# Stick-breaking attention: the order of two steps on ScalarE and of two on TensorE

## The chip, the cores and the metric

The kernel runs on one core of a Trainium2 chip. The time is the device time of one launch in microseconds, as the median of several runs. A core has five engines that run side by side, each through its own list of instructions in order: TensorE (matrix products; PE in the profile, PEld for its weight loads), VectorE (DVE), ScalarE (ACT), GpSimd (POOL) and SyncE (SP, which starts transfers). They meet through semaphores: an instruction adds one when it is done, and another engine waits until a count is reached. TensorE writes into PSUM, eight banks of 512 f32 numbers for each of 128 partitions.

## The reference, cut to what matters

The program is a chain of four mixing layers. The change touches one part of the third: stick-breaking attention, 8 heads of 64 numbers over 1024 positions.

```
def stick_breaking(q, k, v):
    ...
    for blk in range(S // SB_BLOCK):
        ...
        z = jnp.einsum('bthd,bshd->bhts', qf[:, q0:kend], kf[:, :kend]) * scale
        ...
        strict = s_idx < t_idx
        log_beta = jax.nn.log_sigmoid(z)
        log_one_minus = jnp.where(strict, jax.nn.log_sigmoid(-z), 0.0)
        suffix = lax.cumsum(log_one_minus, axis=3, reverse=True) - log_one_minus
        w = jnp.where(strict, jnp.exp(log_beta + suffix), 0.0)
        outs.append(jnp.einsum('bhts,bshd->bthd', w, vf[:, :kend]))
```

For each query t and key s before it, the weight is exp(z minus the sum of softplus(z) over the keys from s up to t). Everything ahead of this part (projections of the third layer, its retention) and behind it (output projection, fourth layer) stays as it is.

## The kernel before, in words

The work of this part is cut into 48 blocks. A block is a pair of heads `a` (4 pairs), a group `g` of 512 queries (2 groups) and 128 keys `kb`. Where the keys lie inside the query group, the queries ahead of them are left out: a block is 512, 384, 256 or 128 queries wide (`512 - cols_of(n)`; below: width 4, 3, 2 or 1). Both heads are computed together, so one instruction of VectorE or ScalarE on scores of width 4 has 2 x 512 = 1024 elements for each partition.

`stick_chain` and the loop below it (lines 752 to 762) set the order of the blocks. The widths in that order are 4 4 4 3 4 2 4 1 4, then three times 4 3 4 2 4 1 3 4 2 4 1 4, of which the last turn's end runs out with 3 2 1 behind it. All blocks with `kb > 0` are `decays` (40 of the 48): the sum already accumulated for their queries has to be multiplied by a decay. The blocks with `kb >= 4 * g` (32 of them) get a mask.

Block n goes through these steps, on these engines:

1. `stick_scores(n)`, TensorE, line 1508: the mask (line 1518, two small bf16 products, where there is one) and the scores (line 1521) into one of three pairs of PSUM banks (`z_at(n)`, n modulo 3). It waits until the weights of block n - 3 have been read out of those banks (`weight_ready`).
2. min, VectorE, line 2961: the scores, cut off at 30, into `SE`. It waits for the scores.
3. exp, then ln(1 + x), ScalarE, lines 2135 and 2139, on `SE` in place. The exp waits for the min.
4. max, VectorE, line 2953 (`stick_softplus`): the softplus into `SSP`. It waits for the ln.
5. `stick_sums(n)`, TensorE, line 1525: the running sums over the keys, added to the scores in PSUM (line 1530), and, for a block in `decays`, the totals over its keys into the single bank `T_BANK` (line 1537). The first waits for the max, the second also until the decay of the block before in `decays` has been read out of that bank (`decay_out`).
6. `stick_weights(n)`, ScalarE, line 2116: exp of that, out of PSUM, into `SPT`. It waits for the sums.
7. `stick_decay(n)`, ScalarE, line 2123: exp of minus the totals, for blocks in `decays`.
8. `stick_decayed(n)`, VectorE, line 2939: the accumulated sum times the decay.
9. `stick_values(n)`, TensorE, line 1540: the weights times the values, into one bank.
10. `stick_add(n)`, VectorE, line 2926: add that to the accumulated sum; at the last block of a query group one product more, into `MIXT`.

The order is written out by hand, as one loop over n on each of the three engines:

- TensorE (line 1553): scores(n), sums(n - 2), values(n - 3).
- ScalarE (line 2131): exp(n), weights(n - 2), ln(n), decay(n - 2).
- VectorE (line 2955): add(n - 4), min(n), max(n - 1), decayed(n - 3).

`f` and `v` issue through `InOrder.op` (line 163): each instruction of ScalarE and of VectorE waits for the one before it on its engine, and the profile puts them all at line 169. Behind the part, `layer_done` (line 1562) releases all engines into `boundary(3)`. No DMA is issued by the loops. SyncE fills weight slots as they come free, and GpSimd waits for `layer_done`.

Of the kernel before, what the change touches and what calls it, by code (L numbers as in the profile page):

```python
# [173 lines left out]
def build(nc, A, out):  # L174

    with ExitStack() as ctx:
# [158 lines left out]
        def view(eng, key):  # L335

            u, _, _, place = units[key]
            eng.wait_ge(unit_ready, u + 1)
            return place
# [10 lines left out]
        def landed(eng, *keys):  # L350

            for key in keys:
                _, b, n, _ = units[key]
                eng.wait_ge(ev[b], n)
# [63 lines left out]
        for n in range(2):  # L418
            add(f"h_out{n}", rows_by_tile(h_out, 512 * n, 512 * n + 512))
        chunk_at = {name: n for n, (name, _) in enumerate(chunks)}  # L420

        def slot_view(n):
# [208 lines left out]
        def top_units(m):  # L631
            return 5 if has_tail(groups[m][0]) else 4
# [8 lines left out]
        for m in range(len(groups) - 1):  # L641
            done = last_step[m] - 2
            for u in range(top_units(m + 1)):
                n = done - top_units(m + 1) + 1 + u
# [110 lines left out]
        blocks = []  # L755
# [9 lines left out]
        def cols_of(n):  # L765
            _, g, kb = blocks[n]
            return P * max(0, kb - 4 * g)

        def z_at(n):
            o = 512 * (2 + 2 * (n % 3))  # L770
            return PS[:, o:o + 1024].rearrange("p (h c) -> p h c", h=2)
# [46 lines left out]
        def _(pe):  # L818
# [689 lines left out]
            def stick_scores(n):  # L1508

                a, g, kb = blocks[n]  # L1510
                c0 = cols_of(n)
                w = 512 - c0
                z = z_at(n)
                if n >= 3:
                    pe.wait_ge(weight_ready, n - 2)
                if kb >= 4 * g:
                    for i in range(2):
                        mm(z[:, i, 0:P], STRICT_BF, ID_BF, start=True, stop=False, skip_group_check=True)
                for i in range(2):
                    r = 64 * i  # L1520
                    last = mm(z[:, i, 0:w], SKT[r:r + 64, a, kb * P:(kb + 1) * P], SQT[r:r + 64, a, 512 * g + c0:512 * g + 512],
                              start=kb < 4 * g, stop=False, skip_group_check=True)
                    last.then_inc(z_ready, 1)

            def stick_sums(n):

                w = 512 - cols_of(n)
                pe.wait_ge(sp_ready, n + 1)
                for i in range(2):
                    last = mm(z_at(n)[:, i, 0:w], LOWER, SSP[n % 2][:, i, 0:w], start=False, stop=True, skip_group_check=True)  # L1530
                last.then_inc(logs_summed, 1)
                if n in decays:
                    k = decays.index(n)
                    if k:
                        pe.wait_ge(decay_out, k)
                    for i in range(2):
                        last = mm(T_BANK[64 * i:64 * i + 64, 0:w], ONES[:, 0:64], SSP[n % 2][:, i, 0:w], start=True, stop=True)
                    last.then_inc(total_ready, 1)

            def stick_values(n):  # L1540

                a, g, kb = blocks[n]
                w = 512 - cols_of(n)
                pe.wait_ge(weight_ready, n + 1)
                if n:
                    pe.wait_ge(block_taken, n)
                for i in range(2):
                    h = 2 * a + i
                    last = mm(B_BANK[64 * i:64 * i + 64, 0:w], SV[:, kb, h * SD:(h + 1) * SD], SPT[n % 2][:, i, 0:w], start=True, stop=True)
                last.then_inc(block_ready, 1)  # L1550

            pe.wait_ge(lower_ready, 1)
            for n in range(len(blocks) + 3):
                if n < len(blocks):
                    stick_scores(n)
                if 2 <= n < len(blocks) + 2:
                    stick_sums(n - 2)
                if n >= 3:
                    stick_values(n - 3)
            pe.wait_ge(block_taken, len(blocks))  # L1560
# [132 lines left out]
        def _(act):  # L1693
# [191 lines left out]
            for u, name in enumerate(e_halves):  # L1885
                what, n = divmod(u, 2)
# [229 lines left out]
            def stick_weights(n):  # L2116
                w = 512 - cols_of(n)
                act.wait_ge(logs_summed, n + 1)
                if n >= 2:
                    act.wait_ge(block_ready, n - 1)  # L2120
                f(SPT[n % 2][:, :, 0:w], z_at(n)[:, :, 0:w], ACT.Exp).then_inc(weight_ready, 1)

            def stick_decay(n):
                if n in decays:
                    k, w = decays.index(n), 512 - cols_of(n)
                    act.wait_ge(total_ready, k + 1)
                    if k >= 2:
                        act.wait_ge(decayed_acc, k - 1)
                    f(SF[k % 2][:, 0:w], PS[:, 512:512 + w], ACT.Exp, scale=-1.0).then_inc(decay_out, 1)

            for n in range(len(blocks) + 2):
                if n < len(blocks):
                    e = SE[n % 2][:, :, 0:512 - cols_of(n)]
                    act.wait_ge(low_ready, n + 1)
                    f(e, e, ACT.Exp)
                if n >= 2:
                    stick_weights(n - 2)
                if n < len(blocks):
                    f(e, e, ACT.Ln, bias=1.0).then_inc(ln_ready, 1)
                if n >= 2:  # L2140
                    stick_decay(n - 2)
# [99 lines left out]
            for t in range(NL):  # L2241
                for s in range(NS):
                    n = t * NS + s
# [1101 lines left out]
```

## Time and profile before

| | before |
|---|---|
| median of 3 runs | 2767.04 us (2765.52 to 2770.16) |
| the profiled execution | 2770.5 us, span of the core 2768.7 us |
| the stick-breaking part | from 1925.7 to about 2129.8 us of the span |
| TensorE, matmul | 2566.3 us busy, 93% of the span |
| TensorE, weight loads | 1979.2 us, 71% |
| VectorE | 1419.2 us, 51% |
| ScalarE | 1153.6 us, 42% |
| GpSimd | 381.1 us, 14% |
| mean granted TensorE clock | 0.969 of full speed |

A matmul on f32 operands shows as two matmul records, so the two heads give "x4" in a merged row. A row of the timeline has the start in microseconds of the span, the duration, the engine, the line, the operation, the tiles and shapes, how many instructions were merged, and in brackets the idle time before it and what ended that. The end of a matmul is modelled. So the time from the start of one group of matmuls to the start of the next is read here as what the group holds the engine for, where the engine didn't wait between.

### The profile page before, as it was taken

What the parts mean: (1) busy time and instruction counts of PE and PEld (TensorE: products, weight loads), DVE (VectorE), ACT (ScalarE), POOL (GpSimd) and SP (SyncE); (2) the same over time, 40 slices, a digit from 0 to 9 for tenths busy, and PEclk for the clock granted to TensorE, in tenths of its full rate; (3) what the DMA queues carried; (4) which work ended last, traced back from release to release, by engine and by line L of the source; (5) the groups of instructions that cost most, each with busy time, mean ns of one, the idle gap of its engine ahead of it and who ended that gap; (6) DMA issues with size and microseconds to landing.
All of it is one profiled execution on the core that took longest, in us unless ns stands there. A gap on an engine that the chain in (4) does not pass through costs nothing. (4 is left out here: it accounts for less than half of the span.)

```text
span 2768.7 us, 38552 instructions
## 1 busy us (share of the span) xinstructions
PE 2566.3 (93%) x14759; PEld 1979.2 (71%) x14759; DVE 1419.2 (51%) x2283; ACT 1153.6 (42%) x1977; POOL 381.1 (14%) x415
## 2 busy tenths in 40 slices
PE   4999998999999999989999999899998999999787
PEld 3778987877778878933337778786334877798776
DVE  5113265666655514666764723411777547265752
ACT  6112344454454321134443622311767647333662
POOL 1000020010020000046761000000000010004710
PEclk8999999999999999989999999999999999998889
DMA  7430010000112131110002220102000220111012
GB/s 257 174 139 24 18 33 1 1 1 1 62 54 91 47 61 46 32 37 1 1 1 91 92 78 30 59 3 76 1 1 24 84 88 31 38 47 62 1 54 76
DMA packets 87991, 139.73 MB, mean 50 GB/s; under 512 B 19513, under 2 KB 54738, under 8 KB 87682
## 3 DMA queue, kind: packets, MB, share of 16 engines
q1 hardware_dynamic: 70592, 75.90, 8.8%
q0 software_dynamic: 16976, 61.30, 6.2%
q8 instruction: 120, 1.97, 0.3%
q14 instruction: 61, 0.50, 0.1%
q10 hardware_dynamic: 242, 0.07, 0.0%
HBM read 120.47 MB, written 16.78 MB: 50 GB/s over the span
## 5 line engine op out<-in xcount | busy, mean ns | idle before, releaser
L169 ACT ACTIVATE WORK<-PS 128x512 f32<-128x512 f32 (+5 forms) x309 | 152.6, 494 | 659.2 <-PE PS L863 388.7
L863 PE MATMUL PS<-HT_R,W_R 128*128 128x512 f32 (+1 forms) x896 | 334.3, 373 | 0.0
L862 PE MATMUL PS<-WORK_R,W_R 128*128 128x512 f32 (+1 forms) x736 | 271.4, 369 | 0.0
L861 PE MATMUL PS<-WORK_R,W_R 128*128 128x512 f32 (+1 forms) x672 | 250.0, 372 | 14.4 <-DVE W_R L169 9.9
L169 ACT ACTIVATE HT<-PS 128x1024 f32<-128x1024 f32 (+6 forms) x211 | 156.0, 739 | 161.0 <-PE PS L1296 126.4
L989 PE MATMUL PS<-WORK_R,HT_R 128*128 128x512 f32 x528 | 210.3, 398 | 8.8 <-DVE W_R L169 7.5
L863 PE MATMUL PS<-W_R,WORK_R 128*128 128x256 f32 (+3 forms) x704 | 215.2, 306 | 0.0
L990 PE MATMUL PS<-WORK_R,MIXT_R 128*128 128x512 f32 x544 | 214.1, 394 | 0.0
L991 PE MATMUL PS<-W_R,HT_R 128*128 128x512 f32 x528 | 207.4, 393 | 0.0
L862 PE MATMUL PS<-W_R,HT_R 128*128 128x256 f32 (+2 forms) x688 | 206.2, 300 | 0.0
L926 PE MATMUL PS<-BASE,WORK 128*128 128x128 f32 (+1 forms) x1186 | 175.2, 283 | 25.3 <-DVE WORK L169 16.8
L863 PEld LDWEIGHTS PS<-HT_R,W_R 128*128 128x128 f32 x896 | 170.8, 191 | 29.9
L926 PEld LDWEIGHTS PS<-BASE,WORK 128*128 128x128 f32 (+1 forms) x1186 | 137.7, 143 | 54.7 <-issue 17.7
L861 PE MATMUL PS<-W_R,WORK_R 128*128 128x256 f32 (+2 forms) x560 | 169.0, 302 | 2.9 <-issue 1.4
L169 DVE TENSOR_TENSOR W_R<-W,W_R 128x1024 fp32r<-128x1024 f32 (+2 forms) x76 | 86.9, 1165 | 162.7 <-ACT W_R L169 143.5
L861 PEld LDWEIGHTS PS<-WORK_R,W_R 128*128 128x128 f32 x672 | 128.5, 191 | 43.8 <-issue 23.5
L169 DVE COPY WORK<-PS 128x512 f32<-128x512 f32 (+1 forms) x101 | 61.3, 607 | 191.7 <-PE PS L863 103.6
L862 PEld LDWEIGHTS PS<-WORK_R,W_R 128*128 128x128 f32 x736 | 140.6, 191 | 22.4 <-issue 0.5
L169 ACT ACTIVATE MIXT<-PS 128x512 f32<-128x512 f32 (+1 forms) x76 | 43.7, 575 | 262.4 <-PE PS L863 236.3
L169 ACT ACTIVATE WORK<-WORK 128x1024 f32<-128x1024 f32 (+2 forms) x88 | 78.9, 897 | 153.8 <-DVE WORK L169 149.2
L863 PEld LDWEIGHTS PS<-W_R,WORK_R 128*128 128x128 f32 x704 | 134.6, 191 | 3.9
L862 PEld LDWEIGHTS PS<-W_R,HT_R 128*128 128x128 f32 x688 | 132.1, 192 | 2.5
(328 smaller groups left out, 5587.3 us busy)
## 6 DMA issues: line engine op xcount, KB each, us to landing
MIXT<-in_w_mod POOLq DMA_DIRECT2D x8, 2048.0 KB, 8.7
x_scratch<-WORK POOLq DMA_DIRECT2D x24, 512.0 KB, 2.9
WORK<-x_scratch POOLq DMA_DIRECT2D x24, 512.0 KB, 3.6
W<-in_odd_w_in SPq DMA_DIRECT2D x12, 1024.0 KB, 5.2
W<-in_even_w_in SPq DMA_DIRECT2D x5, 2048.0 KB, 7.9
W<-in_w_mod SPq DMA_DIRECT2D x4, 2048.0 KB, 20.8
WORK<-in_x POOLq DMA_DIRECT2D x16, 512.0 KB, 8.7
W<-in_e_w_in SPq DMA_DIRECT2D x6, 1024.0 KB, 5.9
```

The source lines that it names most:

```text
L169: self.last = Signalled(self, issue(*args, **kwargs))
L861: mm(out, a[0], b_[0], start=k == 0, stop=False)
L862: mm(out, a[1], b_[0], start=False, stop=False)
L863: return mm(out, a[0], b_[1], start=False, stop=k == KT - 1)
L926: last = nc.tensor.transpose(bank[0:m, n * P:n * P + a.shape[0]], a, IDENT[0:a.shape[0], 0:a.shape[0]])
L989: mm(bank, high, wh, start=k == 0, stop=False)
L990: mm(bank, low, wh, start=False, stop=False)
L991: last = mm(bank, high, wl, start=False, stop=k == KT - 1)
```

## The change

ScalarE's loop now does the weights of block n - 2 ahead of the exp of block n, so that exp(n) and ln(n) follow one another. TensorE's loop does the sums (and totals) of block n - 2 ahead of the scores of block n. VectorE's loop, all instructions, tiles and waits stay as they are.

```diff
@@ TensorE
             for n in range(len(blocks) + 3):
+                if 2 <= n < len(blocks) + 2:
+                    stick_sums(n - 2)
                 if n < len(blocks):
                     stick_scores(n)
-                if 2 <= n < len(blocks) + 2:
-                    stick_sums(n - 2)
                 if n >= 3:
                     stick_values(n - 3)
@@ ScalarE
             for n in range(len(blocks) + 2):
+                if n >= 2:
+                    stick_weights(n - 2)
                 if n < len(blocks):
                     e = SE[n % 2][:, :, 0:512 - cols_of(n)]
                     act.wait_ge(low_ready, n + 1)
                     f(e, e, ACT.Exp)
-                if n >= 2:
-                    stick_weights(n - 2)
-                if n < len(blocks):
                     f(e, e, ACT.Ln, bias=1.0).then_inc(ln_ready, 1)
                 if n >= 2:
                     stick_decay(n - 2)
```

## Rows read from the trace of the kernel before

**Rows 1.** Windows: start:end, length, busy PE, PEld, DVE, ACT, POOL, clock, DMA share, GB/s.

```profile
1927.50:2120.70 193.20, 175.75 (x752) 66.05 (x750) 138.36 (x179) 133.61 (x174) 0.00 (x0) 1.00 0.03 12
```

**Rows 2.** Timeline: the second and the last block's masked scores, TensorE.

```profile
1927.52 0.40 PE L1518 MATMUL PS<-BF 128*128 128x128 bf16 x2
...
2120.73 0.28 PE L1518 MATMUL PS<-BF 128*128 128x128 bf16 x2
```

**Rows 3.** Waits in 1925 to 2132: who waited for whom, total, times, longest.

```profile
PE PS L1518 <- ACT HT L169: 13.9, 18, 1.6
```

**Rows 4.** Timeline, the part's first rounds.

```profile
1925.72 1.86 PE L1521 MATMUL PS<-WORK 64*128 64x512 f32 x4 [0.64 <-DVEq L2920]
...
1929.80 1.23 DVE L169 TENSOR_SCALAR HT<-PS 128x1024 f32<-128x1024 f32 x1 [0.95 <-PE PS L1521]
1931.13 1.23 DVE L169 TENSOR_TENSOR HT<-PS,HT 128x1024 f32<-128x1024 f32 x1
...
1932.41 1.98 PE L1530 MATMUL PS<-HT 128*128 128x512 f32 x4 [1.83 <-DVE HT L169]
...
1933.72 1.06 ACT L169 ACTIVATE HT<-HT 128x1024 f32<-128x1024 f32 x1 [0.46 <-DVE HT L169]
...
1934.87 1.02 ACT L169 ACTIVATE HT<-PS 128x1024 f32<-128x1024 f32 x1
...
1935.95 0.29 PE L1518 MATMUL PS<-BF 128*128 128x128 bf16 x2 [1.55 <-ACT HT L169]
```

**Rows 5.** Timeline, two rounds in the middle: TensorE's groups, one VectorE min.

```profile
1988.20 1.98 PE L1530 MATMUL PS<-HT 128*128 128x512 f32 x4
...
1990.12 1.08 PE L1537 MATMUL PS<-HT,ONES 128*64 128x512 f32 x4
...
1991.03 0.60 PE L1549 MATMUL PS<-HT,WORK 128*64 128x256 f32 x4
...
1991.56 1.13 PE L1521 MATMUL PS<-WORK 64*128 64x512 f32 x4
...
1992.62 0.71 PE L1530 MATMUL PS<-HT 128*128 128x128 f32 x4
...
1992.76 1.22 DVE L169 TENSOR_SCALAR HT<-PS 128x1024 f32<-128x1024 f32 x1 [0.66 <-PE PS L1521]
...
1993.26 0.44 PE L1537 MATMUL PS<-HT,ONES 128*64 128x128 f32 x4
...
1993.53 1.03 PE L1549 MATMUL PS<-HT,WORK 128*64 128x512 f32 x4
```

**Rows 6.** Timeline, TensorE: mask and scores of a block of width 1.

```profile
2003.95 0.28 PE L1518 MATMUL PS<-BF 128*128 128x128 bf16 x2
2004.17 0.49 PE L1521 MATMUL PS<-WORK 64*128 64x128 f32 x4
```

**Rows 7.** Groups by form in 1925 to 2132, VectorE: the min, widest and narrowest.

```profile
L169 DVE TENSOR_SCALAR HT<-PS 128x1024 f32<-128x1024 f32 x24 | 29.4, 1225 | 13.9 <-PE PS L1521 13.5
...
L169 DVE TENSOR_SCALAR HT<-PS 128x256 f32<-128x256 f32 x8 | 3.4, 424 | 4.0 <-PE PS L1521 3.9
```

**Rows 8.** The same for ScalarE: exp and ln (HT<-HT); weights and decay (HT<-PS).

```profile
L169 ACT ACTIVATE HT<-HT 128x1024 f32<-128x1024 f32 x48 | 50.7, 1057 | 35.8 <-DVE HT L169 34.9
...
L169 ACT ACTIVATE HT<-PS 128x512 f32<-128x512 f32 x24 | 14.3, 597 | 3.5 <-PE PS L1530 0.9
...
L169 ACT ACTIVATE HT<-HT 128x256 f32<-128x256 f32 x16 | 6.7, 416 | 1.4 <-DVE HT L169 0.8
...
L169 ACT ACTIVATE HT<-PS 128x128 f32<-128x128 f32 x8 | 2.2, 277 | 0.9
```

**Rows 9.** Windows of two stretches where TensorE is idle part of the time.

```profile
1930.00:1935.00 5.00, 2.57 (x8) 0.68 (x4) 4.68 (x4) 4.33 (x5) 0.00 (x0) 1.00 0.67 219
...
1786.00:1788.00 2.00, 1.12 (x4) 0.72 (x4) 1.72 (x5) 0.43 (x1) 0.00 (x0) 0.51 0.02 4
```

**Rows 10.** Timeline, TensorE: the idle time ahead of the second of these.

```profile
1786.32 1.12 PE L926 MATMUL PS<-BASE,WORK 128*128 128x128 f32 x4 [2.56 <-DVE WORK L169]
```

## The prediction

> **What bounds the kernel now.** I read the windows of the part first, then the waits, then the timeline. From the second block's scores to the last block's lie 193.2 us and 46 steps (1927.52 to 2120.73) [rows 2], 4.20 us a step. In them TensorE's matmul records are busy 175.75 us, 91%, VectorE and ScalarE about 70% [rows 1]. TensorE's largest wait is the one ahead of a block's mask, for ScalarE: 13.9 us in 18 of the 32 masked blocks [rows 3]. The first rounds show what it is: exp until 1934.78, weights until 1935.89, scores at 1935.95 [rows 4]. The ring is scores(n), min(n), exp(n), weights(n - 2), scores(n + 1): the weights stand behind the exp in ScalarE's order and free the banks that the next scores need. For width 4 it takes 1.13 + 0.07 + 1.22 + 0.04 + 1.06 + 0.09 + 1.02 + 0.06 = 4.69 us [rows 4, 5]. TensorE's own work on such a block is sums 1.92 (1988.20 to 1990.12), totals 0.91, scores 1.06 (1991.56 to 1992.62), values 0.9 (the 1.03 from 1993.53 less the modelled end that also lies in the scores' 1.13), together 4.8 us [rows 5]. So two bounds lie close together, and the change takes the first away.
>
> A page's rule weighs on how TensorE's 91% is read; the numbers below don't use it. The Trainium skill ("Perfetto Trace Analysis", Identifying the Most-Contended Engine) says that matmul busy time is a poor measure of nearness to the limit and that weight-load share is the better one. Here that is 66.05 of 193.2 us, 34% [rows 1], so by the page TensorE is not at its limit, and a dependency may still set the pace. Who trusts the 91% would expect no loss from a new order.
>
> **The change, part by part.** No instruction, byte or DMA is added or removed, and no queue of SP or GpSimd is passed. Both edits move places in an in-order list.
>
> ScalarE: weights(n - 2) ahead of exp(n). Its wait is now for sums(n - 2), which TensorE does ahead of scores(n). So the weights run beside totals(n - 2), scores(n) and min(n), and cost exp(n) nothing: after the sums' end they need 1.02 us, while the min ends 1.13 + 0.07 + 1.22 us after the scores begin [rows 4, 5]. The old ring is gone. Gain at most TensorE's 13.9 us [rows 3].
>
> TensorE: sums(n - 2) and totals(n - 2) ahead of scores(n). This is where it is decided. sums(n - 2) waits for max(n - 2). VectorE's list, which is unchanged, is min(n - 1), max(n - 2): the max stands behind the min of the block after it, and this min waits for scores(n - 1). Behind the waiting sums now stand scores(n) in TensorE's list, and min(n) and everything of block n waits for these. Before, scores(n) ran in that gap. That gives a ring of one step, scores(n + 1), min(n + 1), max(n), sums(n), totals(n), scores(n + 2). The first round shows its links: min 1929.80, max 1931.13, sums 1932.41, after an idle 1.83 us of TensorE [rows 4]. Before the change only that first round waits so, since scores(n + 2) fills the time.
>
> There is a second branch. totals(n) waits for decay(n - 1), the last item of ScalarE's round n + 1: min(n + 1), exp(n + 1), ln(n + 1), decay(n - 1). It applies where n and n - 1 are both in decays.
>
> Terms, by width 4 and width 1, in proportion between: scores until their semaphore S 1.13 and 0.49, mask 0.22 more (2003.95 to 2004.17) [rows 5, 6]; min M and max X both 1.225 and 0.424 [rows 7] (the max shows the same 1.23 for width 4 [rows 4]); exp and ln E each 1.057 and 0.416, decay D 0.597 and 0.277 [rows 8]; sums U, start to next start, 1.92 and 0.64 (1992.62 to 1993.26), totals T 0.91 and 0.27 [rows 5]. Hops: scores to min 0.07 (1991.56 + 1.13 to 1992.76), min to max 0.10, max to sums 0.05; min to exp 0.04, exp to ln 0.03 (an estimate below the 0.09 between exp and weights), ln to decay 0.10, decay to totals 0.06 [rows 4, 5].
>
> Step = S + mask + 0.07 + M of block n + 1, then the larger of
> - 0.10 + X(n) + 0.05 + U(n)
> - 0.04 + 2 E(n + 1) + 0.03 + 0.10 + D(n - 1) + 0.06
>
> then T(n) if n is in decays. For width 4 throughout, without mask: 2.42 + 3.30 + 0.91 = 6.63 us, against 4.8 before.
>
> One turn of twelve (widths 4 3 4 2 4 1 3 4 2 4 1 4): 5.46, 5.94, 4.98, 4.82, 5.41, 4.95, 5.74, 5.89, 5.85, 5.41, 5.86, 6.63, sum 66.9. ScalarE's branch is the larger in four of them (1 to 3, 3 to 4, 2 to 4, 1 to 4). The nine opening steps (5.94, 5.72, 6.37, 6.06, 5.89, 5.85, 5.41, 5.86, 6.63) give 53.7. The third turn ends at a block of width 3 and gives 66.7, and one step of 5.0 is left. Together 53.7 + 66.9 + 66.9 + 66.7 + 5.0 = 259.2 us, 5.6 a step, against 193.2: +66.0.
>
> The ends: the second scores still run at the low clock at the start (VectorE's min starts 2.28 us after 1927.52, where the terms give 1.42): +0.9. At the end the sums and totals of block 45 (1.49 + 0.70, by the same proportion) no longer lie behind the last scores; between 0 and 2.2 comes back, I take 1.5. Net +65.4 us. The part has all engines to itself: all wait at its end for one semaphore, so the whole of it is on the path. The profiled execution would go from 2770.5 to 2835.9 us; it lies 3.5 above the median of the runs, so for the median 2767.0 + 65.4 = 2832.4, and I say 2832.
>
> The other waits are covered. add(n - 3), ahead of min(n + 1), needs values that TensorE finished a step before; VectorE's whole round, min, max and two products of about 0.7, is 3.9 us of 6.6. The values behind the scores end about 2.2 us into the step, the sums begin at 3.8. If the cover went, 0.7 us for that step.
>
> Bounds: without ScalarE's branch the steps sum to 243.9, so +50 us, 2817. Without T too (totals that cost nothing, which no row suggests) 20 us less. If the sums held TensorE 0.2 us less a block where they are waited for than where they follow the scores, 9 us less. Above: each hop 0.1 longer in 46 steps and four places is 18 us more, which the rows of such hops don't support; 5 us do.
>
> **Rivals.**
>
> 1. The clock falls (8%). TensorE would be idle some 1.8 us at a stretch in each step. With one such gap and 2.57 us of work in 5 us the clock stayed at 1.00; with 2.56 us idle ahead of 1786.32 it stood at 0.51, its lower level, 1.2 GHz [rows 9, 10]. At 1.2 GHz the scores of width 4 take 1.86 instead of 1.13 [rows 4]; sums and totals streaming twice as long add about 1.7 and 0.85, so 3.3 us for width 4, 2.5 for the mean width of 3. In a quarter of the steps: +29, 2861. In all: +115. The gaps lie between the two cases seen, nearer the first. The Trainium skill ("TensorE: Matmul & The Clock Gate", Part 1: The HAM clock gate) says that the throttled state is the default and activity lifts it, and warns of kernels that idle between groups; the trace agrees that both states occur.
>
> 2. Faster (2%): the removed wait is the only thing that changes. If each max(n - 2) were done when TensorE reaches its sums, the steps would fall to TensorE's own work, 2767 - 14 = 2753. For it: in the old steady state the sums never wait. Against it: this is so because scores(n) are ahead of them. The point from which it decides is whether max(n - 2) can end before scores(n) are issued without delaying min(n); with VectorE's order of min(n - 1), max(n - 2) a gap of M + X + hops = 2.6 us opens at width 4, and only about 0.9 of values fills it.
>
> 3. TensorE stays the bound, no change (1%): 2767. Its 91% speaks for it; the ring, longer than its work on every step of width 4, against.
>
> 4. Decay branch hidden or shorter hops (9%): 2817 to 2822, worked out above.
>
> **How the numbers follow.** Forecast 80%, 2832, with 2822 to 2845 by hops and ends. The range takes in case 4 and the lighter half of case 1: 2817 to 2858. About 0.2%, 5.5 us, is what a measurement here can tell from no change; only rivals 2 and 3 reach there. Faster 0.02, same 0.01, slower 0.97.
>
> **What would show it.** The part lasts some 269 us instead of 204. TensorE's wait for ScalarE ahead of the mask is gone, and waits of about 1.8 us for VectorE stand ahead of line 1530 in nearly all of 46 rounds, with some for ScalarE ahead of line 1537 where a narrow block precedes a wide one. Durations of each form stay. VectorE and ScalarE fall to some 52% busy in the part. Wrong would be: sums that start right behind the values; scores that wait for weights as before; a part under 250 us; a clock well under 1.00.

## The result, and the profile after

The changed kernel takes 2858.72 us (median of 4 runs, 2857.13 to 2862.57) against 2767.32 us before: a ratio of 1.0326, 95% interval 1.0311 to 1.0342, or 91 us slower. The profiled execution took 2862.57 us with a span of 2860.8 us.

The page, part 1, after: TensorE's matmul records add up to 36.6 us more in the same number of instructions; VectorE, ScalarE and GpSimd are busy as before to 1.3 us.

```profile
PE 2602.9 (91%) x14759; PEld 1983.0 (69%) x14759; DVE 1417.9 (50%) x2283; ACT 1154.4 (40%) x1977; POOL 381.4 (13%) x415
```

The windows of the part (columns as in rows 1): the whole part, and from the second block's scores to the last block's.

```profile
1925.60:2220.40 294.80, 218.79 (x800) 73.06 (x800) 144.54 (x191) 138.64 (x184) 0.00 (x0) 0.90 0.03 10
1927.30:2212.90 285.60, 210.72 (x760) 69.89 (x758) 139.25 (x180) 135.67 (x177) 0.00 (x0) 0.89 0.02 8
```

The part takes 294.8 us where it took 204.1: 90.7 us, the whole loss. The second row answers to [rows 1]: 285.6 us where there were 193.2, and a clock of 0.89 where it was 1.00. VectorE and ScalarE do the same work in it. The waits (who waited for whom, total, times, longest), 1925 to 2225:

```profile
DVE HT L169 <- PE PS L1521: 133.8, 48, 4.8
...
PE PS L1530 <- DVE HT L169: 61.2, 46, 2.7
ACT HT L169 <- PE PS L1530: 51.0, 33, 3.3
...
PE PS L1537 <- ACT HT L169: 14.0, 12, 1.6
```

The wait of [rows 3], matmuls of the mask for ScalarE, is gone. In its place the running sums wait for VectorE in 46 of 48 blocks, and the totals for ScalarE in 12. One step at full clock, a block of width 4 behind one of width 3, in the timeline:

```profile
1996.80 0.28 PE L1518 MATMUL PS<-BF 128*128 128x128 bf16 x2
...
1997.00 1.13 PE L1521 MATMUL PS<-WORK 64*128 64x512 f32 x4
...
1998.20 1.23 DVE L169 TENSOR_SCALAR HT<-PS 128x1024 f32<-128x1024 f32 x1 [1.77 <-PE PS L1521]
...
1999.56 0.96 DVE L169 TENSOR_TENSOR HT<-PS,HT 128x768 f32<-128x768 f32 x1
...
2000.57 1.56 PE L1530 MATMUL PS<-HT 128*128 128x384 f32 x4 [1.44 <-DVE HT L169]
...
2002.06 0.87 PE L1537 MATMUL PS<-HT,ONES 128*64 128x384 f32 x4
...
2002.86 0.11 PEld L1518 LDWEIGHTS PS<-BF 128*128 128x128 bf16 x2 [0.60 <-issue]
```

This is the ring in one piece: the scores of block n + 1, its min, the max of block n, the sums and totals of block n, and the next mask at 2002.86. It takes 6.06 us; the terms gave 5.94. The max cannot start at 1998.20, though its ln was done long before, because the min is ahead of it in VectorE's list.

What the terms did not hold is the clock. TensorE's sums of width 4, from the start of the part:

```profile
1932.27 3.35 PE L1530 MATMUL PS<-HT 128*128 128x512 f32 x4 [2.69 <-DVE HT L169]
...
1939.64 3.63 PE L1530 MATMUL PS<-HT 128*128 128x512 f32 x4 [2.69 <-DVE HT L169]
...
1946.67 1.98 PE L1530 MATMUL PS<-HT 128*128 128x512 f32 x4 [1.44 <-DVE HT L169]
```

The same four products take 3.35 to 3.63 us behind idle stretches of 2.69 us, and 1.98 behind 1.44 (before: 1.98 behind 1.83 [rows 4]). Two windows later in the part show that this comes and goes:

```profile
1980.00:2000.00 20.00, 15.32 (x44) 4.54 (x44) 8.95 (x11) 8.41 (x12) 0.00 (x0) 0.74 0.00 1
2000.00:2020.00 20.00, 15.98 (x66) 5.64 (x66) 10.31 (x14) 10.11 (x14) 0.00 (x0) 1.00 0.00 0
```

In the first TensorE is as busy as in the second, but with 44 matmul records instead of 66: half of that window was spent at the lower level (0.74 lies midway between 0.5 and 1.0). It begins in a step that has two idle stretches, one ahead of the sums and one ahead of the totals of a block of width 1:

```profile
1978.61 0.71 PE L1530 MATMUL PS<-HT 128*128 128x128 f32 x4 [1.33 <-DVE HT L169]
...
1980.94 0.69 PE L1537 MATMUL PS<-HT,ONES 128*64 128x128 f32 x4 [1.62 <-ACT HT L169]
...
1981.56 2.08 PE L1521 MATMUL PS<-WORK 64*128 64x512 f32 x4
```

The scores behind them take 2.08 us instead of 1.13. Such a step, 1.33 us idle and then 1.62, comes four times in the part (its totals start at 1980.94, 2052.37, 2123.82 and 2195.76), and the work behind it ran at the lower level all four times. So the wait for the decay seems to cost more than its own length; e5 and e8 below bear on that.

### The profile page after: what moved, and what is told of

Same layout as the page of the kernel before. It is cut to its first block and busy times, and to the rows that moved or that the text cites. A ratio compares the mean times of both kernels' runs of the same rounds, so it can differ in the third digit from the quotient of the medians.

```text
span 2860.8 us, 38552 instructions
## 1 busy us (share of the span) xinstructions
PE 2602.9 (91%) x14759; PEld 1983.0 (69%) x14759; DVE 1417.9 (50%) x2283; ACT 1154.4 (40%) x1977; POOL 381.4 (13%) x415
## 5 line engine op out<-in xcount | busy, mean ns | idle before, releaser
L169 ACT ACTIVATE HT<-HT 128x1024 f32<-128x1024 f32 (+3 forms) x136 | 105.1, 773 | 102.0 <-DVE HT L169 96.7
L1530 PE MATMUL PS<-HT 128*128 128x512 f32 (+3 forms) x192 | 85.3, 571 | 61.3 <-DVE HT L169 61.2
```

The costliest lines, as they stand in the source:

```text
L169: self.last = Signalled(self, issue(*args, **kwargs))
```

## The experiments

Nine kernels ran, in three groups (e1 to e4, e5 to e8, e9), each group beside runs of the kernel before on the same chip (medians 2770.95, 2768.97 and 2768.94 us). I compare ratios to that. A difference of 0.001 is 2.8 us. Ratios come from all runs, lengths and clocks of the part from the one profiled execution of each kernel.

| kernel | median us | ratio to before | interval |
|---|---|---|---|
| changed kernel | 2858.72 | 1.0326 | 1.0311 to 1.0342 |
| e1, ScalarE's edit alone | 2763.58 | 0.9976 | 0.9967 to 0.9986 |
| e2, TensorE's edit alone | 2884.05 | 1.0409 | 1.0395 to 1.0423 |
| e3, change + max first | 2816.96 | 1.0169 | 1.0155 to 1.0182 |
| e4, change + extra product | 2839.93 | 1.0247 | 1.0233 to 1.0261 |
| e5, change + decay early | 2833.96 | 1.0229 | 1.0213 to 1.0245 |
| e6, change + max first + decay early | 2776.83 | 1.0026 | 1.0017 to 1.0036 |
| e7, e1 + decay early | 2755.51 | 0.9950 | 0.9938 to 0.9962 |
| e8, e4 + decay early | 2822.41 | 1.0194 | 1.0180 to 1.0208 |
| e9, e7 + max first | 2766.86 | 0.9991 | 0.9982 to 1.0000 |

**e1, ScalarE's edit alone.** TensorE's loop as in the kernel before:

```diff
             for n in range(len(blocks) + 3):
-                if 2 <= n < len(blocks) + 2:
-                    stick_sums(n - 2)
                 if n < len(blocks):
                     stick_scores(n)
+                if 2 <= n < len(blocks) + 2:
+                    stick_sums(n - 2)
```

> Only ScalarE's edit; TensorE keeps scores(n), sums(n - 2), values(n - 3). My theory: all of the loss is TensorE's edit. The weights then end about 1.06 + 1.92 + 0.06 + 1.02 us after the scores begin, before TensorE has done sums, totals and values, so its 13.9 us of waiting ahead of the mask go and nothing takes their place: 2753 to 2760 us. Rival (exp and ln held behind the weights are late for the max, and that costs): 2767 to 2790 us. Rival (ScalarE's edit carries part of the loss): above 2790 us.

Measured: 0.9976, some 6.6 us faster than before; the median, 2763.58, lies 3.6 above the expected interval, where the kernel before lay 3.9 above its own earlier median. So this half of the change is a small gain, and both rivals fall. TensorE's waits in the part, 1925 to 2130:

```profile
PE PS L1537 <- ACT HT L169: 8.0, 11, 0.9
...
PE PS L1518 <- ACT HT L169: 2.1, 4, 1.1
```

The 13.9 us of [rows 3] are 2.1, and a new wait of 8.0 stands ahead of the totals: the decay now comes behind exp and ln in one stretch. I had not named that one.

**e2, TensorE's edit alone.** ScalarE's loop as in the kernel before:

```diff
             for n in range(len(blocks) + 2):
-                if n >= 2:
-                    stick_weights(n - 2)
                 if n < len(blocks):
                     ...
                     f(e, e, ACT.Exp)
+                if n >= 2:
+                    stick_weights(n - 2)
+                if n < len(blocks):
                     f(e, e, ACT.Ln, bias=1.0).then_inc(ln_ready, 1)
```

> Only TensorE's edit; ScalarE keeps exp(n), weights(n - 2), ln(n), decay(n - 2). My theory: the ring scores, min, max, sums, totals stays, and the branch over decay(n - 1) grows by the weights between exp and ln (0.4 to 1.0 us) where it is the longer one. The steps at full clock sum to 274.6 us instead of 259.2, so about 15 us above the changed kernel: 2868 to 2880 us. Rival (only the ring over the max counts, totals wait for nothing): as the changed kernel, 2859 us. Rival (the loss was ScalarE's): near 2767 us.

Measured: 1.0409, so 0.0083 or 23 us above the changed kernel, where 15 were expected; the median, 2884.05, lies 4 us above the expected interval. The part's waits:

```profile
PE PS L1530 <- DVE HT L169: 57.6, 44, 2.7
PE PS L1537 <- ACT HT L169: 29.0, 15, 2.8
```

The wait for the decay went from 14.0 to 29.0 us, which is the 15 us of the sum. The mean clock over its part (1923.96 to 2242.70) was 0.85, where the changed kernel's was 0.90. That may be the other 8 us; no run separates it. Both rivals fall: the loss was TensorE's edit, and the branch over the decay counts.

**e3, the change with VectorE's max first.**

```diff
             for n in range(len(blocks) + 4):
                 ...
+                if 1 <= n <= len(blocks):
+                    stick_softplus(n - 1)
                 if n < len(blocks):
                     ...
                     v.tensor_scalar(SE[n % 2][:, :, 0:w], z_at(n)[:, :, 0:w], SOFTPLUS_IS_Z, None, ALU.min).then_inc(low_ready, 1)
-                if 1 <= n <= len(blocks):
-                    stick_softplus(n - 1)
```

> The changed kernel, with VectorE's max(n - 1) put ahead of min(n). My theory: the ring exists only since the max stands behind the next block's min. With the max first, sums(n - 2) wait for nothing of block n - 1, the waits for VectorE ahead of line 1530 go, and the clock stays at 1.00. A new ring is min, exp, ln, max, next min: 4.8 us for width 4, 177 us plus hops over 46 steps, under TensorE's own 178 us and more. 2750 to 2785 us. Rival (sums and totals ahead of the scores cost by themselves, since the scores come out later): above 2820 us.

Measured: 1.0169. This missed by 32 us. The waits for the max did go, from 61.2 to 5.6 us, but the totals now waited 35.0 us for ScalarE (TensorE's waits, 1925 to 2180):

```profile
PE PS L1537 <- ACT HT L169: 35.0, 19, 3.0
PE PS L1530 <- DVE HT L169: 5.6, 5, 2.5
```

In the timeline of this kernel: exp and ln of the next block (one merged row), then one merged row with the decay and, behind it, the weights of the block of width 2; and the totals.

```profile
2018.57 2.15 ACT L169 ACTIVATE HT<-HT 128x1024 f32<-128x1024 f32 x2 [2.39 <-DVE HT L169]
...
2020.83 1.31 ACT L169 ACTIVATE HT<-PS 128x512 f32<-128x512 f32 x2
...
2021.47 0.65 PE L1537 MATMUL PS<-HT,ONES 128*64 128x256 f32 x4 [2.38 <-ACT HT L169]
```

The totals start in the middle of the merged ScalarE row, 0.64 us after its start: the decay is its first item (0.60 us), and it had stood behind exp and ln. My expectation had left out the prediction's own second branch: with the first ring cut, the second alone still ties scores(n + 1) to scores(n + 2). The clock did not stay at 1.00 either: over the part (1924.50 to 2177.30) it was 0.90, as in the changed kernel, so the 47 us that e3 still loses are the second branch and the lower clock together. The rival, that TensorE's order costs by itself, could not be told from this until e6.

**e4, a product in the idle time.** Ahead of the wait for the max, one f32 product of 512 columns into banks that the next scores overwrite, behind a wait for those banks to be free; it adds nothing to the output.

```diff
                 w = 512 - cols_of(n)
+                if n + 2 < len(blocks):
+                    if n >= 1:
+                        pe.wait_ge(weight_ready, n)
+                    mm(z_at(n + 2)[:, 0, 0:512], LOWER, SQT[:, 0, 0:512], start=True, stop=True, skip_group_check=True)
                 pe.wait_ge(sp_ready, n + 1)
```

> The changed kernel, with one product more (f32, 512 columns, about 0.9 us) on TensorE ahead of each wait for the max, into the banks that the next scores overwrite. My theory: the 26 us above my sum are the clock, which falls in the idle stretches. The product fills a stretch that is idle anyway and keeps the clock near 1.00 in the part: 2826 to 2840 us. Rival (the 26 us are longer hops or a ring term that I mis-sized, and the clock is a bystander): 2859 us or, as the product then adds to the ring, more. Rival (the product is too little to hold the clock): 2855 to 2865 with the clock as before.

Measured: 1.0247, so 0.0079 or 22 us faster than the changed kernel, by adding work. The part:

```profile
1925.60:2202.00 276.40, 244.50 (x892) 82.02 (x890) 144.71 (x191) 138.61 (x184) 0.00 (x0) 0.98 0.03 11
```

It takes 276.4 us at a clock of 0.98, 18 us less than the changed kernel's. The loss against before is 68 us by the ratio and 72 by the part's length in the profiled execution; the prediction's sum, at full clock, was 65. The wait for ScalarE ahead of the totals is 14.0 us as in the changed kernel; the clock rose, and the idle time ahead of the sums fell from 61.2 us to 16.6, since the product stands in it. Both rivals fall.

**e5 and e8, the decay early.** ScalarE's decay right behind the weights, in the changed kernel (e5) and in e4 (e8):

```diff
                 if n >= 2:
                     stick_weights(n - 2)
+                    stick_decay(n - 2)
                 ...
                     f(e, e, ACT.Ln, bias=1.0).then_inc(ln_ready, 1)
-                if n >= 2:
-                    stick_decay(n - 2)
```

> The changed kernel, with ScalarE's decay(n - 2) moved from behind ln(n) to right behind weights(n - 2). My theory: of the two branches only the one over the max is left. At full clock the steps sum to 243.9 instead of 259.2 us, so 15 us less, if the clock's share stays what it was: 2838 to 2850 us. Rival (the branch over the decay is a minor one, already covered): 2855 to 2862 us. Rival (the exp, now behind the decay, comes later and lengthens the ring): above 2862 us.

> The changed kernel with the decay right behind the weights and the extra product ahead of each wait for the max. It has only the branch over the max, at a clock near 1.00. My theory: 15 us below the run with the extra product alone (2840 us): 2820 to 2830 us. Rival (the extra product stands on the ring in the short steps, once the decay does not wait any more): 2830 to 2845 us.

Measured: e5 1.0229, 27 us below the changed kernel where 15 were expected, so below the interval given; e8 1.0194, 15 us below e4, as the sum has it (259.2 less 243.9), and inside the interval given. TensorE's waits in e5 (1925 to 2200), and the part of e8:

```profile
PE PS L1530 <- DVE HT L169: 66.4, 47, 2.7
```

```profile
1925.60:2183.00 257.40, 237.65 (x886) 80.40 (x884) 144.30 (x192) 138.76 (x185) 0.00 (x0) 1.00 0.03 9
```

The wait for ScalarE ahead of the totals is gone from both. e8 is the cleanest test of the sum: one branch, at a clock of 1.00. The row leaves out the first 1.9 us of e8's part, whose first scores start at 1923.68. With them it is 259.1 us at a mean clock of 0.99, which is 55 more than before; the prediction's lower bound was 50. In e5 the further 12 us fit the clock, 0.96 in 1925 to 2180 against 0.90 in the changed kernel's part: the steps with two idle stretches are gone, and it fell less often. That the clock is what makes up these 12 us is inferred from e8, in which they don't appear.

**e6, both rings cut, with TensorE's new order kept.** The edits of e3 and e5 together.

> The changed kernel with both moves: max(n - 1) ahead of min(n), and the decay right behind the weights. My theory: with the max first alone (2817 us) the branch over the decay was left as a ring of its own. With both cut, sums and totals wait for nothing of the next block, and TensorE's own work of some 180 us with the ring min, exp, ln, max bounds the part: 2752 to 2775 us, clock 0.99 or more in the part. Rival (sums and totals ahead of the scores cost by themselves): stays above 2800 us.

Measured: 1.0026, 2776.83 us, 2 us above the expected interval, and 83 us below the changed kernel. TensorE's order, sums ahead of scores, is in it unchanged; so nearly the whole loss comes from the two places in VectorE's and ScalarE's lists that the sums and totals have to wait behind, together with the clock that falls in those waits (0.98 in this part). The rival falls; e9 measures what is left of it. What TensorE still waits for:

```profile
PE PS L1530 <- DVE HT L169: 18.7, 25, 2.4
```

**e7, ScalarE's edit with the decay early.** e1 with the edit of e5.

> ScalarE's edit alone, TensorE's order as in the kernel before, and the decay right behind the weights too. In the run with ScalarE's edit alone TensorE still waited 8.0 us for ScalarE ahead of line 1537, for decays behind the ln. My theory: these waits go: 6 to 8 us below that run, 0.995 of the kernel before, some 2757 us where before is 2770. Rival (exp and ln come later and the max waits for them, so the sums do): equal to that run or slower, 2764 to 2775 us.

Measured: 0.9950 (0.9938 to 0.9962), 2755.51 us, 13 us faster than before and the fastest of all, as expected (0.995). The 8.0 us ahead of the totals are gone, nothing waits there (1925 to 2125):

```profile
PE PS L1518 <- ACT HT L169: 2.8, 8, 1.1
PE PS L1530 <- DVE HT L169: 1.8, 1, 1.8
```

**e9, e7 with the max first.** It differs from e6 in TensorE's order alone, and from e7 in VectorE's alone.

> The fastest version so far (ScalarE: weights, decay, exp, ln; TensorE's order as before) with VectorE's max(n - 1) ahead of min(n). It differs from the run with both rings cut (1.0026 of the kernel before) in TensorE's order alone. My theory: with the scores issued first, the 18.7 us that TensorE still waited there for VectorE ahead of line 1530 are filled, and TensorE's own work bounds the part: 0.994 to 0.998 of the kernel before, 2752 to 2763 us where before is 2769. Rival (those 18.7 us belong to the ring min, exp, ln, max, next min, whatever TensorE's order): 1.001 to 1.004.

Measured: 0.9991, between the two expected intervals (up to 0.998, and from 1.001), so neither holds alone. Against e6 it is 0.0035, 10 us, faster: that is what sums ahead of scores cost by themselves. Against e7 it is 0.0041, 11 us, slower: that is what the max ahead of the min costs. TensorE's waits:

```profile
PE PS L1518 <- ACT HT L169: 8.8, 13, 2.6
PE PS L1521 <- ACT HT L169: 2.9, 3, 1.0
PE PS L1530 <- DVE HT L169: 1.2, 1, 1.2
```

With the scores first the 18.7 us ahead of the sums are filled, and 11.7 us ahead of the scores, for the weights, come in. A likely reading is that a min behind the max, which waits for the ln, delays exp and all behind it; no run separates that.

## Why the prediction was right or wrong

- **Sign and mechanism: right.** The ring over the max is in the timeline link by link, and the waits stand ahead of lines 1530 and 1537 as foretold. They are shorter than foretold, 61.2 us in 46 rounds or 1.33 each, where some 1.8 were expected. e1 and e2 show that the loss belongs to TensorE's edit, e3, e5 and e6 that it lies in the two branches.
- **The sum at full clock: right, a little low.** +65 us forecast with both branches; e4 gives 68 by the ratio and 72 by the part, at a clock of 0.98. +50 with one branch; e8 gives 55 in the part at 0.99. 5 us over 46 steps are 0.11 us a step.
- **The decay branch: right in size** (15 us forecast; from e4 to e8 15 by the ratios, 18 by the parts' lengths), though I then forgot it in e3's expectation.
- **"The clock falls (8%)": wrong.** This is the step that failed: the forecast put the clock's term at nothing and gave the rival that has it 8%. I placed the gaps between the case that held the clock and the one that lost it, "nearer the first", on one gap of 1.8 us in each step. The trace has 2.69 us in the first two rounds and up to 2.08 later, most of the others are shorter than 1.8, and the clock fell all the same, above all where the totals wait and a second gap stands in the same step. It was 0.89 between the second and the last scores instead of 1.00. A mean of 0.90 over 294.8 us means some 59 us at the lower level, a fifth of the part. e4 puts the price at about 20 us (18 by the parts, 22 by the ratios), and the loss of 91 less the sum's 65 leaves 26. The price given for that rival, +29 us for a quarter of the steps and 2861 us, is close. So the likeliest case should have been the ring with a falling clock.
- **The time: near, by a wide range.** 2832 was 27 us low, and 2822 to 2845, the range by hops and ends, missed. The measured median lies 0.7 us above the upper end of 2817 to 2858; taken as the ratio on the 2767.04 us known then it is 2857.2, just inside. That it comes so close is owed to the rival's lighter half, which the range took in, and not to the forecast's own terms.
- **The old ring's wait goes: right**, and worth 6.6 us by itself (e1), less than the 13.9 given as the most: 2.1 us of that wait are left, and 8.0 us of new waits stand ahead of the totals.
- **Faster, or no change: rightly set low.** VectorE's unchanged order decided, as the rival's text said. TensorE's 91% in [rows 1] was no sign that it would stay the bound.

## What to carry to other kernels

Before moving a step ahead of another in one engine's list, follow what it waits for through the other engines' unchanged lists: if it stands there behind an item of the next round, the move closes a ring of one step, however early its own inputs are ready. Here each item was one place too late in a list, and the cost was the rest of the chain, laid bare in each of 46 steps. Where a new chain leaves TensorE idle in every step, as here for up to 2.7 us at a time, a sum worked out at full clock is a lower bound, and the lower clock belongs in the forecast as a term. When a swap is made of two edits, time each alone: here one gained 0.24% (0.5% with the decay moved too) and the other lost 4%.

## What the runs showed of the hardware

- Adding one product a step to idle TensorE time, in e4, made the kernel 22 us faster by the ratios: the part's clock rose from 0.90 to 0.98. In e8 it was 1.00 from 1925.6 us on, at 237.65 us of busy records in 257.4.
- Work at 1.2 GHz followed idle stretches of 2.69 us (sums of width 4 in 3.35 to 3.63 us instead of 1.98), and also shorter ones: in all four steps with 1.33 and then 1.62 us idle. Three steps of the changed kernel with a single stretch of 2.07 to 2.08 us ahead of the sums (at 1994.97, 2064.28 and 2135.72) kept 1.98 us; in e5 sums behind a stretch of 2.07 us, at 1986.57, took 3.00. So the length of the last stretch doesn't tell the level of the work behind it. What tips it in a given step is open.
